# Attention products with both halves of the weights in one matmul, their four output parts added after a trip through DRAM

## The reference, cut to what matters

```python
def stick_breaking_block(start, q, k, v):
    ...
    a = jnp.where(visible, jnp.exp(jax.nn.log_sigmoid(z) + excl), 0.0)
    return jnp.einsum('bhqk,bkhd->bqhd', a, v)

def dsa_block(start, q, k, v, q_idx, k_idx, w_idx, k_top):
    ...
    p = jax.nn.softmax(logits, axis=-1)
    return jnp.einsum('bhqk,bqkhd->bhqd', p, vg)

def hybrid_mixer(h, w_in, b_gate, w_branch_sb, w_branch_dsa, w_out, k_top):
    ...
    merged = gate_sb * (o_sb @ w_branch_sb) + gate_ds * (o_ds @ w_branch_dsa)
    return merged @ w_out
```

## Time and profile before

| | us |
|---|---|
| median of 3 runs | 1741.37 (1740.12 to 1743.99) |
| the profiled execution | 1746.8 |
| its span, first to last instruction | 1745.0 |
| attention block, SB steps with filling | about 240 to 722 |
| DSA steps | about 722 to 918 |
| branch, output, MLP | 918 to the end |

### The profile page before, as it was taken

The page is one execution under the profiler, slowest core; times in us unless marked ns, Lnnn a source line. Parts: engine busy times, 40 slices in busy tenths (PEclk is TensorE's granted clock), DMA queues, the critical chain, the costliest instruction groups (busy, mean ns, idle before and its releaser), DMA issues. The chain is left out here.

```text
span 1745.0 us, 23454 instructions
## 1 busy us (share of the span) xinstructions
PE 1638.4 (94%) x8360; PEld 1384.4 (79%) x8360; DVE 1245.4 (71%) x1966; ACT 851.5 (49%) x1650; POOL 539.7 (31%) x332
## 2 busy tenths in 40 slices
PE   4999899999999999889889999989999999999997
PEld 4889888799877777777777878768888878888885
DVE  5287798888988989687873435785454548777878
ACT  5266555555445545576751133555555543333334
POOL 1111254555434435321102450475545510000000
PEclk6999999999999999998989999999999999999999
DMA  4564434344233233355304443243444365443434
GB/s 172 155 194 124 128 120 134 108 137 114 89 106 107 92 106 107 91 134 135 86 1 163 139 169 121 72 158 133 145 149 174 136 229 217 157 159 131 169 138 103
DMA packets 101372, 231.23 MB, mean 133 GB/s; under 512 B 11192, under 2 KB 25848, under 8 KB 101256
## 3 DMA queue, kind: packets, MB, share of 16 engines
q1 hardware_dynamic: 100680, 227.64, 40.7%
q0 software_dynamic: 576, 2.10, 0.7%
HBM read 155.83 MB, written 73.86 MB: 132 GB/s over the span
## 5 line engine op out<-in xcount | busy, mean ns | idle before, releaser
L710 PE MATMUL bk<-x_hi,w_hi 128*128 128x512 f32 (+2 forms) x832 | 308.7, 371 | 1.2 <-PEq L353 1.2
L710 PE MATMUL bk<-x_lo,w_hi 128*128 128x512 f32 (+2 forms) x832 | 299.3, 360 | 0.0
L710 PE MATMUL bk<-x_hi,w_lo 128*128 128x512 f32 (+2 forms) x832 | 298.5, 359 | 0.0
L666 POOL TENSOR_TENSOR pt_lo<-a_buf,pt_hi 128x512 fp32r<-128x512 f32 (+3 forms) x104 | 138.4, 1347 | 193.0 <-ACT pt_hi L930 192.8
L334 POOL TENSOR_TENSOR w_lo<-w_raw,w_hi 128x1024 fp32r<-128x1024 f32 x53 | 130.4, 2460 | 190.9 <-ACT w_hi L330 190.7
L1087 DVE TENSOR_SCALAR_CACHE_REDUCE counted<-sc,small 128x272 uint8<-128x272 f32 (+6 forms) x217 | 182.5, 891 | 0.9
L1674 PE MATMUL bank<-v_hi,f_hi 128*128 128x512 f32 x448 | 174.3, 389 | 0.0
L1674 PE MATMUL bank<-v_hi,f_lo 128*128 128x512 f32 x448 | 174.3, 389 | 0.0
L1674 PE MATMUL bank<-v_lo,f_hi 128*128 128x512 f32 x448 | 174.3, 389 | 0.0
L710 PEld LDWEIGHTS bk<-x_hi,w_lo 128*128 128x128 f32 x832 | 158.5, 191 | 17.6
L710 PEld LDWEIGHTS bk<-x_hi,w_hi 128*128 128x128 f32 x832 | 159.1, 191 | 16.1 <-issue 1.3
(11 more groups left out here) (228 smaller groups left out, 3861.0 us busy)
## 6 DMA issues: line engine op xcount, KB each, us to landing
w_raw<-w_units SPq DMA_DIRECT2D x57, 512.0 KB, 3.7
f_raw<-f_d SPq DMA_DIRECT2D x28, 1024.0 KB, 5.0
u_raw<-w_units SPq DMA_DIRECT2D x32, 512.0 KB, 4.8
f_d<-f_s SPq DMA_DIRECT2D x64, 256.0 KB, 2.2
b<-w_units SPq DMA_DIRECT2D x16, 1024.0 KB, 8.3
f_d<-c SPq DMA_DIRECT2D x48, 256.0 KB, 2.1
k_hi<-k_d SPq DMA_DIRECT2D x32, 260.0 KB, 5.6
k_lo<-k_d SPq DMA_DIRECT2D x32, 260.0 KB, 6.1
```

The lines of the kernel that those rows point to most:

```text
L666: pool.tensor_tensor(pt_of(pt_lo, j, tiles), raw, pt_of(pt_hi, j, tiles).bitcast(F32), ALU.subtract).then_inc(sb_lo, 1)
L710: mm = pe.matmul(pj[b][:, 0:c1 - c0], w[:, s, kt, :], a[:, kt, c0:c1], start=kt == 0 and k == 0, stop=kt == KT - 1 and k == 2)
```

## The change

It makes one matmul of the two in each slot. `pt_hi` and `pt_lo` become the two halves of one tile `pt` (128 x 2 x columns), so that a slot moves 2 x 256 columns past the same stationary `v_hl`, into a whole PSUM bank: high and low weights times high and low values stand in four parts, 128 rows by 2 x 256. Nothing is summed across weights in PSUM any more.

All outputs up to k = 55 (K_LAST = 56), DSA's too, are copied by ScalarE as 128x512 into `o_st`, which is now one buffer where there were two of half the size, and spilled to an `o_d` twice as large. At the seven entries of RELOAD (steps +2, +6, +11, +16, +21, +37, +53, for the head pairs 0 to 6) SP loads four parts: the first two at that step, the third a step later, the fourth another step later, the last three all into `o_raw[1]`, each after POOL has added the one before. POOL makes three additions for a pair. ScalarE's reload (rounding, pairs 0 to 3 only) stands four steps after the RELOAD step; POOL's rest behind it, and SP's loads for pairs 1 to 3 wait for the rest of the pair before (`or_lo`). For the DSA pairs 4 to 6 the sum is made in `o_pair`, and VectorE's scale_pair waits for it (`or_sum`), at steps +26, +42 and +58. Only the last pair of heads (k = 56 to 63) keeps the way through ScalarE's copy, now with three additions on VectorE in place of one.

ScalarE's output(k) moves ahead of round_weights in its turn. work(j) counts 190 for a slot, not 245, which moves some projection pieces between SB steps; their total is the same.

```diff
-RELOAD = [NJ // 2 + 6 + 10 * p_ for p_ in range(4)]
-PAIR_AT = [NJ // 2 + 16 * (p_ + 1) + 4 for p_ in range(3)] + [NJ + 1]
+RELOAD = [(NJ // 2 + step_, p_) for step_, p_ in ((2, 0), (6, 1), (11, 2), (16, 3), (21, 4), (37, 5), (53, 6))]
+PAIR_AT = [NJ // 2 + 16 * (p_ + 1) + 10 for p_ in range(3)] + [NJ + 1]
+K_LAST = 4 * H + 24
...
                 def spill(k):
                     sp.wait_ge(o_free, k + 1)
-                    sp.dma_start(o_d[k // 4, :, pair_cols(k)], o_st[:, k % 2]).then_inc(o_spilled[k % 2], 16)
+                    sp.dma_start(o_d[k // 4, :, :, pair_cols(k)].rearrange("s p c -> p s c"), o_st[:]).then_inc(o_spilled, 16)
+
+                def load_piece(n, x):
+                    p = RELOAD[n][1]
+                    s, half = divmod(x, 2)
+                    if x == 0:
+                        sp.wait_ge(o_spilled, 16 * 8 * (p + 1))
+                        if n == 0:
+                            in_dram(U_BRANCH - 1)
+                        if 1 <= p < 4:
+                            sp.wait_ge(or_lo, p)
+                    elif n or x > 1:
+                        sp.wait_ge(or_sum, 3 * n + x - 1)
+                    dst = o_raw[1] if x else o_raw[0] if p < 4 else o_pair[p - 4]
+                    for g in range(2):
+                        sp.dma_start(dst[DH * g:DH * g + DH], o_d[2 * p + g, s, DH * half:DH * half + DH, :]).then_inc(or_in, 16)
...
+                    for n, (step, p) in enumerate(RELOAD):
+                        if step <= j < step + 3:
+                            for x in ((0, 1), (2,), (3,))[j - step]:
+                                load_piece(n, x)
...
+                    for n, (step, p) in enumerate(RELOAD):
+                        if step < j <= step + 3:
+                            x, whole = j - step, o_raw[0] if p < 4 else o_pair[p - 4]
+                            pool.wait_ge(or_in, 128 * n + 32 * (x + 1))
+                            if x > 1:
+                                pool.wait_ge(or_sum, 3 * n + x - 1)
+                            pool.tensor_tensor(whole[:], whole[:], o_raw[1][:], ALU.add).then_inc(or_sum, 1)
+                        if j == step + 4 and p < 4:
                             pool.wait_ge(or_hi, p + 1)
...
-                        for w in (hi, lo):
-                            mm = pe.matmul(dst, v_hl[0:r, g % 2, slot, :], w[0:r, cols], start=slot == 0 and w is hi,
-                                           stop=slot == o + 1 and w is lo)
+                        mm = pe.matmul(dst, v_hl[0:r, g % 2, slot, :], whole[0:r, :, cols], start=slot == 0, stop=slot == o + 1)
...
                     act.wait_ge(pv_done, k + 1)
-                    if g < H:
-                        if k >= 2:
-                            act.wait_ge(o_spilled[k % 2], 16 * (k // 2))
-                        act.copy(o_st[:, k % 2], o_part(k)).then_inc(o_free, 1)
+                    if k < K_LAST:
+                        if k:
+                            act.wait_ge(o_spilled, 16 * k)
+                        act.copy(o_st[:], o_part(k)).then_inc(o_free, 1)
...
-                    for p in range(4):
-                        if j == RELOAD[p] + 3:
-                            reload(p)
+                    for n, (step, p) in enumerate(RELOAD):
+                        if j == step + 4 and p < 4:
+                            reload(n, p)
...
                 def scale_pair(p):
                     if p < 3:
-                        dve.wait_ge(o_free, 4 * H + 8 * (p + 1))
-                    else:
+                        dve.wait_ge(or_sum, 3 * [q for _, q in RELOAD].index(4 + p) + 3)
+                    else:
+                        dve.wait_ge(or_sum, 3 * len(RELOAD))
...
+                def add_rest(k):
+                    n, r = k - K_LAST, DH * (k // 4 % 2)
+                    dst = o_pair[3][r:r + DH, pair_cols(k)]
+                    dve.wait_ge(top_done, n + 1)
+                    dve.tensor_tensor(dst, dst, o_part(k)[0:DH, 1], ALU.add).then_inc(bottom, 1)
+                    dve.wait_ge(bottom, 2 * n + 1)
+                    dve.tensor_tensor(dst, dst, o_part(k)[DH:P, 0], ALU.add).then_inc(bottom, 1)
+                    dve.wait_ge(bottom, 2 * n + 2)
+                    dve.tensor_tensor(dst, dst, o_part(k)[DH:P, 1], ALU.add).then_inc(o_free, 1)
```

54 lines of the change are left out of this document (17 added, 37 removed).

## The result

The changed kernel takes **1843.46 us** (median, 1842.1 to 1846.5), the kernel before beside it 1742.16: a ratio of **1.0584, 95% interval 1.0566 to 1.0603**, or 101 us more. I had forecast 1804, with a range of 1772 to 1830. The direction was right, the size fell short by 39 us.

The account below looks back on a forecast made before the run. TensorE bounds SB; in DSA, TensorE, VectorE and ScalarE form a ring. Span 1745.0 - 8 + 52.6 + 4 + 13 + 1 = 1807.6, 62.6 more; carried to the median 1741.4, 1804 us, range 1772 to 1830.

Parts of the forecast that it names:

- the chain of pairs 0 to 3: DSA steps: 26.9 us reload cycles against 10.5 to 13.1 us of steps; ScalarE's roundings late, +52.6, other loads +4.
- the DSA pairs: Pairs 4 to 6: VectorE's scale_pair waits 4 to 5.5 us each for sums, +13; rest of DSA 0.
- the end: Block's end: two more VectorE additions of 0.424 us after the last product, +1 us.
- part 1: TensorE's products: one matmul for two saves 0.16 us a product, 4.8 us over SB's 30, nothing in DSA.
- The copy first: SB: output copy ahead of ScalarE's roundings frees the bank earlier; TensorE's 3.9 us of waits go.
- The filling table: SB steps: the new work(j) count only moves projections, 0 us.
- SB in sum: SB stretch: -4.8 - 3.9 + 1 (VectorE taking some back) = -8 us, between -15 and -2.
- part 2: ScalarE's output copy in SB: -3.9 us; longer copy and single o_st's wait for the previous spill hidden.
- rival C: DSA: waits idle TensorE, restarting at 1.2 GHz; heads' loads late behind SP's blocked queue, some 4; 1820 us, chance 0.14.
- A: Reloads: SP gets far enough ahead, so ScalarE's roundings wait for nothing; 1732 us, chance 0.08.
- B: Chain: faster loads, cycle 25.5 us, +47, scale_pair waits vanish; 1778 us, 1782 with one scale wait; chance 0.17.
- D: Pairs 4 to 6: POOL's nine additions, 2.375 us each, hold VectorE up, 21 us; 1825 us, chance 0.03.

Follow-up runs that it names:

- e1: Kernel before with only ScalarE's output copy moved first in its turn: 1731.19 us, ratio 0.9934.
- e2: The change with DSA outputs (k from 32) back on their earlier way, so pairs 4 to 6 make no DRAM trip: 1792.36 us, ratio 1.0288.
- e16: e2 with 245 ns table, output 31's own buffer, eight reload DMAs at once into four buffers, steps +9, +19, +28, +41: 1730.09 us, ratio 0.9937.
- e17: Kernel before with output copy first for SB outputs only, on the same chip as e16: 1731.13 us, ratio 0.9938.
- e7: The change with the old filling table (245 ns for a slot in work(j), not 190): 1837.37 us, ratio 1.0538.
- e12: e1 with the new filling table (190 ns for a slot, not 245), products as before: 1733.14 us, ratio 0.9957.
- e5: e2 with reloads at +2, +14, +26, +38, later parts three and six steps later, rounding ten steps behind the first load: 1744.54 us, ratio 1.0001.
- e4: The change with a second o_st for odd DSA outputs (k from 33): 1830.13 us, ratio 1.0497.
- e8: The change with spills issued by ScalarE, and first loads of pairs from 4 on waiting for the previous pair's additions: 1829.82 us, ratio 1.0496.
- e11: The change with scale_pair three steps later (+29, +45, +61): 1843.08 us, ratio 1.0582.
- e13: The change with both edits of e10 and e11, POOL issuing the loads and scale_pair three steps later: 1834.48 us, ratio 1.0512.
- e14: The change with third and fourth parts of pairs 4 to 6 neither loaded nor added: 1819.39 us, ratio 1.0430.
- e10: The change with the four parts' loads issued from POOL's queue, no longer by SP: 1849.24 us, ratio 1.0624.

## Why the prediction was wrong, and where it was right

Put together from the ratios: before to e1, -11.5; e1 to e2, +61.6; e2 to the change, +51.5; in sum 101.6. Divided the same way, the forecast of 62.6 was 48.6 for SB and the chain of pairs 0 to 3 (-8 + 52.6 + 4), against 50.1 measured, and 14 for the DSA pairs and the end (13 + 1), against 51.5. So the whole miss of 39 us lies in the second. That the first came out within 2 us is luck in part: the order gave 7.6 us more than I counted, the table took 4 to 8 that I put at nothing, and one matmul for two gave 2.3 in place of 4.8.

**One matmul for two** (part 1: -4.8). A slot costs what I said. The timeline of TensorE after, the same five slots that took 1.48 us before (508.61 to the next operation at 510.09):

```profile
513.04 1.62 PE L821 MATMUL bk<-pt,v_hl 16*128 16x512 f32 x5
514.50 0.31 PE L771 MATMUL bk<-k_hi,q_st 128*128 128x328 f32 x1
```

1.46 us for them, not 1.32; the two late starts that I counted as saved are not. Other groups of slots save up to 0.08 us. Over the products of SB the starts give 2.3 us, and the beginnings of DSA in six traces 3.5. Right in sign and somewhat too large, and the time as a whole doesn't show it (e16 against e17).

**The copy first** (-3.9). Wrong in size: -11.5. In the sum I had only TensorE's waits for `o_st`, 3.9 us; SB got 5.5 shorter, and the gaps and the lower clock in the head where SB meets DSA were another 4.7 (24.0 to 19.3).

**The filling table** ("0"). Wrong: it costs 8 us in the change (e7), and perhaps 4 in the kernel before (e12, with overlapping intervals). "Only moves projections" is no price: where they leave TensorE idle for longer, that time and a longer stretch at the lower clock are. So SB in sum was forecast at -8 and came to between +1 and -5 in the traces of the change's SB code; with the old table it was -9.1 (e7).

**The chain of pairs 0 to 3** (52.6 + 4). Right. Additions mostly 7.0 us apart (forecast 2.4 + 4.5), first load to third addition as counted, cycles of 27.4, 26.8 and 30.9 us in e2 against 26.9. e1 to e2 is 61.6 us, of which the table is 4 to 8; that leaves 54 to 58 for 56.6, and e5 gives 50 of it back by distance alone. In the change itself the forecast's places show a shift: ScalarE's waits at the rounding were 8.14, 13.38, 0 and 4.91, where I had 9, 15, 14 and 11. The missing ones stand one instruction earlier:

```profile
814.99 0.59 ACT L959 COPY o_st<-bk 128x512 f32<-128x512 f32 x1 [11.31 <-DMA o_d<-o_st]
816.89 1.04 ACT L977 CAST o_hi<-o_raw 128x1024 fp32r<-128x1024 f32 x1
```

The sums came 27.2, 32.1 and 31.5 us apart, so the last rounding was at 848.4 and not 837.2. In the middle cycle the first addition waited 11.57 us for its loads, and 6.95 in e2: a DSA spill stood in front of them in SP's queue. In the last one the second addition came 11.4 us behind the first, with the next head's eight loads issued just ahead of the third part; it was 10.8 in e2 too, so that is not the spills'. The roundings themselves waited 26.4 us for 49 forecast (39.5 in e2).

**The DSA pairs** (13 for the waits of scale_pair, 0 for the rest, +1 at the end): **the step that failed.** It cost 51.5. VectorE's waits themselves were near the forecast, 4.74, 4.98 and 1.21 us for "4 to 6 three times". What I left out:
- The single `o_st` in DSA steps. In part 2 I had called it hidden, for SB steps of over 7 us, and never asked again for DSA steps of 2.62 us, where two outputs follow each other by one step and a spill's landing takes 2.6 us and its issue waits for SP. 15 us (e4, e8).
- SP's queue. I named what is queued behind SP's waits only in rival C ("a late loading of heads behind SP's blocked queue, some 4"). Chains of pairs 4 to 6 block spills and heads' loads as well as VectorE: with VectorE's wait taken away the time stayed and the others grew (e11), with both taken away it fell by 12.5 us (e13). The length of these chains is worth 27 us (e14), of which I had 13.
- The end: from the last exponent to the first branch matmul it took 13.3 us, and 8.5 in e2, where TensorE was at its full clock and not at 0.65. Against before (11.7) it is the +1 that I gave; against e2 it is 4.8.

These three make 47 of the 51.5, if they add, and the traces speak against a clean sum. The change's span is 48.6 us longer than that of e2. Of this 4.3 lie ahead of DSA, where the code is the same and the clock fell at two places more in the change; 3.0 lie in the first three heads, 35.1 in the last five (144.0 against 108.9) and 4.8 at the end. In these last five heads e14 took 25.9 us less than the change and e4 11.9, together more than the 35.1, so the two overlap. How the 51.5 us divide among them stays open.

**The rivals.** A fell: ScalarE's rounding waited. B (1782) has too little of the same. C (1820) pointed to the clock and to late heads' loads, and was the nearest in its mechanism; granted clocks of 0.63 to 0.77 are there. How much of the time they cost was not separated, since every run that takes waits away gives the clock back too. D (1825), the nearest in number, fell by its mechanism: there are 21 additions of POOL, and VectorE's 64 low parts of 512 columns in DSA took 688 ns in the mean before and after. One of them beside an addition took the 0.69 of the earlier trace rows; POOL's and VectorE's timelines:

```profile
911.45 2.36 POOL L693 TENSOR_TENSOR o_pair<-o_pair,o_raw 128x1024 f32<-128x1024 f32 x1 [36.89 <-DMA o_raw<-o_d]
...
913.04 0.69 DVE L1203 TENSOR_TENSOR pt<-bk,pt 128x512 fp32r<-128x512 f32 x1 [1.04 <-ACT pt L942]
```

## What to carry to other kernels

An engine that only issues DMAs is a queue like any other. Once one of its DMAs waits for arithmetic, everything behind it inherits the wait, so list what stands there (spills, the next head's loads) and price each, and price a single buffer anew in each stretch with another length of step. A chain whose length can be added up from rows can be given distance: e5 got 50 us back from step numbers alone. And don't add waits up as costs: 48 us of waits for spills were worth 15 us, since most of them lay behind a chain that set the pace anyway. Split a change that reorders as well as restructures: here the order alone was worth 11 us, and the rest cost 113.

## What the runs showed of the hardware

- The same gap of TensorE (2.6 us at 262 us) was followed by a granted clock of 0.50, that is 1.2 GHz, in four of twelve traces and by 1.00 in eight. The Trainium skill (TensorE: Matmul & The Clock Gate, "Part 1: The HAM clock gate") has the clock halve when TensorE goes idle; the traces agree that it halves, and show that the same gap does it in one execution and not in the next. In the same four traces it fell again behind a gap of 1.7 to 1.8 us, after matmuls had run at 1.00 for one to two us.
- A first slot of 16 rows followed by one of 128 costs about the same extra in one matmul as in two: the five slots took 1.46 against 1.48 us, the first two of them 0.76 against 0.77.
- ScalarE can issue a spill: its 56 issues in e8 took 0.37 us each in the median, SP's in the change 0.43, and the kernel was as fast as e4.
- Loads issued by POOL made the chain longer: in e10 an addition ends 8.2 us behind the one before it in its pair in the mean (7.5 in the median), in the change 7.4 (7.1). The longest distance is 11.4 us in both.
